# Gate and up projections as Strassen products over pairs of feed-forward tiles, in a two-layer decoder trunk

## The reference, cut to what matters

```python
D_MODEL, SEQ, DEPTH, N_META, D_FF = 1024, 1024, 2, 16, 2816
def swiglu(h, w_gate, w_up, w_down):
    return (jax.nn.silu(h @ w_gate) * (h @ w_up)) @ w_down
# h: 16 meta tokens, then the 1024 tokens of x
for layer in range(DEPTH):
    mix = attn_recurrent_mixer(h, ...) if layer % 2 == 0 else multiscale_pool(h, ...)
    h = layer_norm(ALPHA * h + mix, ln_mix_g[layer], ln_mix_b[layer])
    h = layer_norm(ALPHA * h + swiglu(h, w_gate[layer], w_up[layer], w_down[layer]), ln_ffn_g[layer], ln_ffn_b[layer])
return h[:, N_META:]
```

## Time and profile before

| | |
|---|---|
| median of 3 runs | 2736.35 us (2734.56 to 2738.01) |
| profiled execution, its own time | 2737.52 us |
| its span, first to last instruction | 2735.8 us |
| first gate/up matmul of the trunk | at 1060.1 us |
| last matmul of the last down projection | at 2716 us |
| mean granted TensorE clock | 0.96 of full speed |

### The profile page before, as it was taken

The page is one execution under the profiler, slowest core; times in us unless marked ns, Lnnn a source line. Parts: engine busy times, 40 slices in busy tenths (PEclk is TensorE's granted clock), DMA queues, the critical chain, the costliest instruction groups (busy, mean ns, idle before and its releaser), DMA issues.

```text
span 2735.8 us, 36593 instructions
## 1 busy us (share of the span) xinstructions
PE 2602.8 (95%) x14303; PEld 2217.5 (81%) x14303; DVE 1292.4 (47%) x2469; ACT 843.7 (31%) x1385; POOL 1077.6 (39%) x638
## 2 busy tenths in 40 slices
PE   7899999699999987999999999999999999999996
PEld 6789999668778876889888777888878788888885
DVE  6789995878776431333333332332322332232224
ACT  3674221333333222322222322322323232332221
POOL 1432222655444423443333433444434344445442
PEclk9999999689999998999999998999999999999998
DMA  3101220323322243232323322233323233333431
GB/s 129 32 17 58 91 74 13 100 85 105 93 85 91 72 142 116 70 93 78 101 71 92 93 75 79 77 99 101 92 62 93 64 90 108 93 94 107 119 105 47
DMA packets 276470, 232.96 MB, mean 85 GB/s; under 512 B 10448, under 2 KB 257296, under 8 KB 276304
## 3 DMA queue, kind: packets, MB, share of 16 engines
q1 hardware_dynamic: 268112, 222.13, 27.3%
q10 hardware_dynamic: 8192, 8.52, 0.9%
HBM read 217.91 MB, written 12.71 MB: 84 GB/s over the span
## 4 chain that ended last, share of the span: by engine, by line
PE 58%; DMA 1%; POOL 1%; ACT 1%; DVE 1%; issue 0%; POOLq 0%; SPq 0%; ACTq 0%; DVEq 0%
PE banks L1819 34%; PE banks L1835 19%; PE banks L1852 1%; PE banks L1857 1%; PE banks L1869 1%; DMA draw<-in_w_down 1%; PE banks L1543 1%; POOL wL L1738 1%; POOL dL L1745 0%; DMA raw<-in_w_up 0%; ACT wH L1913 0%; ACT dH L1919 0%; DVE y L2019 0%; DVE y L1521 0%; PE banks L1854 0%
## 5 line engine op out<-in xcount | busy, mean ns | idle before, releaser
L1738 POOL TENSOR_TENSOR wL<-raw,wH 128x2048 fp32r<-128x2048 f32 x88 | 406.3, 4617 | 596.2 <-ACT wH L1913 596.2
L1819 PE MATMUL banks<-hL,wH 128*128 128x512 f32 (+1 forms) x1760 | 620.4, 352 | 15.9 <-ACT hid L1928 13.5
L1819 PE MATMUL banks<-hH,wL 128*128 128x512 f32 (+1 forms) x1760 | 619.4, 352 | 0.0
L1819 PE MATMUL banks<-hH,wH 128*128 128x512 f32 (+1 forms) x1760 | 617.2, 351 | 0.0
L1999 DVE TENSOR_TENSOR hid<-hid,banks 128x512 f32<-128x512 f32 (+1 forms) x110 | 64.3, 585 | 759.6 <-PE banks L1819 654.8
L1819 PEld LDWEIGHTS banks<-hL,wH 128*128 128x128 f32 x1760 | 332.8, 189 | 65.4 <-ACT hid L1928 15.1
L1819 PEld LDWEIGHTS banks<-hH,wL 128*128 128x128 f32 x1760 | 332.7, 189 | 46.3
L1819 PEld LDWEIGHTS banks<-hH,wH 128*128 128x128 f32 x1760 | 333.2, 189 | 45.0
L1745 POOL TENSOR_TENSOR dL<-draw,dH 128x1024 fp32r<-128x1024 f32 x88 | 220.9, 2510 | 371.9 <-ACT dH L1919 371.8
L2019 DVE TENSOR_TENSOR y<-y,banks 128x512 f32<-128x512 f32 (+1 forms) x340 | 233.1, 686 | 219.8 <-PE banks L1835 218.8
L1835 PE MATMUL banks<-dH,hidL 128*128 128x512 f32 (+1 forms) x748 | 303.9, 406 | 2.3 <-issue 2.3
(11 more groups left out here) (235 smaller groups left out, 4316.4 us busy)
## 6 DMA issues: line engine op xcount, KB each, us to landing
raw<-in_w_gate SPq DMA_DIRECT2D x88, 512.0 KB, 4.7
raw<-in_w_up SPq DMA_DIRECT2D x88, 512.0 KB, 6.1
draw<-in_w_down SPq DMA_DIRECT2D x88, 512.0 KB, 3.5
w_out_part<-in_w_out SPq DMA_DIRECT2D x64, 512.0 KB, 4.0
va<-in_w_in SPq DMA_DIRECT2D x10, 1024.0 KB, 5.4
va<-in_x SPq DMA_DIRECT2D x8, 512.0 KB, 4.9
vg_scratch<-y ACTq DMA_DIRECT2D x32, 128.0 KB, 1.7
y<-in_x SPq DMA_DIRECT2D x8, 512.0 KB, 7.6
```

The source lines that it names most:

```text
L1738: nc.gpsimd.tensor_tensor(wL[:, ff % 2, :, :, :].rearrange("p g k f -> p (g k f)"), raw[:, :, :, :].rearrange("p g k f -> p (g k f)"), wH[ ...
L1819: last = nc.tensor.matmul(banks[:, GU + (2 * q + g) % 3, 0:n], wt[:, ff % 2, g, k, :], h[:, k, a:a + n], start=(k == 0 and part == 0), sto ...
```

## The change

For a pair of feed-forward tiles (f = 0, 1) and the two halves of a block's tokens (t), gate and up are each a 2x2 product over the two halves of the width: C[f][t] = A[f][0] B[0][t] + A[f][1] B[1][t]. Eight products of quarter size (four width slices, 264 or 256 tokens) become seven, in Winograd's form: four sums of weight quarters (S1 to S4, VectorE `sum_w`, both weights at once, 128x1024), four sums of token quarters (`sum_t`, once per block), and sums of the products on VectorE out of PSUM (`sum_c11` to `sum_c21`, with ScalarE's `keep_m1` copying the first product out). All seven operands of each side are split in high and low parts: seven `high_w` and `low_w` of 128x1024 per pair, through a ring of three, and seven token operands (`turn`, `high_op`, `low_op`) per block, made while the blocks change: some in the last pair of the old block ("early"), the rest in the first of the new ("late"). The silu now works in place on SBUF, and the multiplication with up (`mult`) has both inputs in SBUF. The meta tokens' halves are eight extra columns in block one, with small copies and subtractions of their own. Weights come as four quarters of a pair, eight transfers of 256 KB. The bands are made over pairs 2 to 8. TensorE's order: the first two products of a pair, the down projection of the pair before, the other five.

```diff
-        def gate_up(ff):
...
+        def bank_free(X):
+            if X < 0:
+                return
+            g, o, part = X // (2 * NO), X // 2 % NO, X % 2
+            pe.wait_ge((m1_kept, c11_made, u2_made, u3_made, u4_made, c12_made, c21_made)[o], 2 * g + part + 1)
...
+        def product(g, o):
...
+            for part in range(2):
+                X = 2 * n + part
+                bank_free(X - 3)
+                for k in range(HK):
+                    for t, (wt, h) in enumerate(((wH, hL), (wL, hH), (wH, hH))):
+                        last = nc.tensor.matmul(banks[:, GU + X % 3, 0:ph.n], wt[:, n % RING, part, k, :], h[:, o, k, 0:ph.n],
```

The order in TensorE's queue:

```diff
+            product(g, 0)
+            if when == "late":
+                turn(new, TO_S1)
+            product(g, 1)
...
+            for j in range(of_pair(g - 1)[0].NJ):
+                down(g - 1, j)
...
+            for o in range(2, NO):
+                product(g, o)
+                if when == "early" and o in (TO_S2, TO_S3):
+                    turn(new, o)
```

The order in ScalarE's queue:

```diff
+            keep_m1(g, 0)
+            keep_m1(g, 1)
+            high_w(g, TO_S2)
...
+            high_w(g, TO_S3)
+            silu(g, 0)
...
+            high_w(g, TO_S1)
...
+            high_hid(g, 0)
+            high_d(2 * g)
...
+            high_w(g, TO_S4)
...
+            high_w(g, TO_22)
...
+            silu(g, 1)
+            if g + 1 < NPAIR:
+                high_w(g + 1, TO_11)
+            high_hid(g, 1)
+            silu(g, 2)
+            if g + 1 < NPAIR:
+                high_w(g + 1, TO_21)
+            high_hid(g, 2)
+            high_d(2 * g + 1)
+            silu(g, 3)
+            high_hid(g, 3)
```

The order in VectorE's queue:

```diff
+            sum_w(g, 1)
+            sum_w(g, 2)
+            sum_w(g, 3)
...
+            sum_c11(g, 0)
...
+            sum_c11(g, 1)
+            mult(g, 0)
...
                 for j in range(of_pair(g - 1)[0].NJ):
                     add(g - 1, j)
+                    if j == 1:
+                        sum_w(g, 4)
...
+            low_hid(g, 0)
+            sum_u2(g, 0)
+            sum_u2(g, 1)
...
+            sum_u3(g, 0)
+            sum_u3(g, 1)
...
+            sum_c22(g, 0)
+            sum_u4(g, 0)
+            sum_c22(g, 1)
+            sum_u4(g, 1)
...
+            mult(g, 1)
+            sum_c12(g, 0)
+            low_hid(g, 1)
+            sum_c12(g, 1)
+            mult(g, 2)
+            sum_c21(g, 0)
+            low_hid(g, 2)
+            sum_c21(g, 1)
+            mult(g, 3)
...
+            low_hid(g, 3)
```

The order in POOL's queue:

```diff
+            low_w(g, TO_S2)
+            low_w(g, TO_S3)
+            low_w(g, TO_S1)
...
+            low_d(2 * g)
+            low_w(g, TO_S4)
+            low_w(g, TO_22)
+            if g + 1 < NPAIR:
+                low_w(g + 1, TO_11)
+                low_w(g + 1, TO_21)
             low_d(2 * g + 1)
```

The order in SP's queue:

```diff
+                sp.wait_ge(s_made, 4 * g + 4)
+                load_quad(g + 1, A11)
+                load_quad(g + 1, A12)
             load_d(2 * g + 1)
+            if g + 1 < NPAIR:
+                sp.wait_ge(w_lo, NO * g + TO_S4 + 1)
+                load_quad(g + 1, A21)
+                sp.wait_ge(w_lo, NO * g + TO_22 + 1)
+                load_quad(g + 1, A22)
                 load_d(2 * g + 2)
```

More of the change, by code:

```diff
@@ L1527, in bias @@
         self.nc.gpsimd.tensor_tensor(self.y[0:n, m, :], self.y[0:n, m, :], self.bb[0:n, :], ALU.add).then_inc(self.biased, 1)
[L1529 to L1563, removed]
@@ L1566 @@
-class Phase:
[L1569 to L1578, removed]
+TO_11, TO_21, TO_S2, TO_S3, TO_S1, TO_S4, TO_22 = range(7)
@@ L1585, in phases, with trunk @@
 def phases():
[L1586 to L1591, removed]
+    blocks = ((0, [0, 1, 2, 3, 4], (1, 3), 264), (0, [5, 6, 7, 8], (5, 7), 256),
+              (1, [1, 2, 3, 4], (1, 3), 256), (1, [5, 6, 7, 8], (5, 7), 256))
+    out, down = [], 0
+    for nth, (layer, tiles, half, n) in enumerate(blocks):
+        out.append(Phase(nth, layer, tiles, half, n, down))
+        down += out[-1].downs
     return out
-def trunk(nc, c, sem, sb, banks, ident, ins, y, hH, hL, out):
+def trunk(nc, c, sem, sb, banks, ident, ins, y, out):
     NW = len(POOL_WINDOWS)
@@ new lines, in down @@
+        def down(g, j):
+            ph, i = of_pair(g)
+            if j == 0:
+                pe.wait_ge(d_lo, 2 * g + 2)
+                pe.wait_ge(hid_lo, hids_to(g, 3))
+            m = ph.tiles[j // 2]
+            n = TILES[m][1]
+            num = ph.down(i, j)
+            if num >= 3:
+                pe.wait_ge(y_added, num - 2)
+            for u in range(2):
+                for part, (wt, h) in enumerate(((dH, hidL), (dL, hidH), (dH, hidH))):
+                    if m == 0:
+                        at = (metaL if h is hidL else metaH)[:, u, :]
+                    else:
+                        half = int(m >= ph.half[1])
+                        a = (m - ph.half[half]) * P
+                        at = h[:, u, half, a:a + P]
+                    last = nc.tensor.matmul(banks[0:n, DN + num % 3, :], at, wt[:, u, (j % 2) * 512:(j % 2 + 1) * 512],
+                                            start=(u == 0 and part == 0), stop=(u == 1 and part == 2))
+            last.then_inc(down_psum, 1)
@@ L1840, in pool_d, with turn_meta @@
+        def turn_meta():
+            for k in range(DC):
+                last = nc.tensor.transpose(banks[:, GU, k * N_META:(k + 1) * N_META], y[0:N_META, 0, k * P:(k + 1) * P],
+                                           ident[0:N_META, 0:N_META])
+            last.then_inc(meta_psum, 1)
         def pool_d(j):
@@ L1871, in pool_mix @@
             last.then_inc(mix_psum, 1)
-        for j in range(FIRST):
-            n0.turn(pe, j)
-        d_made, mixes, turns = [0], [0], [0]
+        d_made, mixes = [0], [0]
+        turn_meta()
+        turn(PH[0], TO_11)
         for g in range(NPAIR):
```

574 lines of the change are left out of this document (383 added, 191 removed).

## The result

The changed kernel takes 3000.11 us (median of four runs, 2986.20 to 3001.83) where the kernel before takes 2736.20 (four runs): a ratio of 1.095, 95% interval 1.0933 to 1.0966, 264 us slower. The profiled execution took 2999.37 us, its span 2997.7. The direction was forecast; the size was not, 103 us with a range to 2910.

A forecast was written before the change was run, and what follows sets the result against it. TensorE bounds the kernel before; after, VectorE's two-SBUF-input operations and POOL's subtractions exclude each other. Periods +40, norms +11, block 1 +10, block changes +36, end +6, start 0: +103, 2839 us; own range 2780 to 2875, with rivals 2700 to 2910.

The forecast's parts named there:

- the flat rule: Matmul spacing nearly flat in width: a half-width matmul costs about 0.75 of a full one, some 400 us more; 1 in 100.
- T: In a pair, counted from TensorE's start on the third product: end of VectorE's last low half of hid, 20.35 us.
- The period without the port: Feed-forward pair if VectorE's operations with two SBUF inputs and POOL's subtractions did not exclude each other (the port): 31.0 us.
- The step that failed: Down projection: the fourth weight sum waits for POOL's fourth low half, T+8.65; the third addition ends at T+10.45.
- the start: Stretch up to the first down projection: 0 us taken, bounds -20 and +10, beginning near 1112 as before.
- the averaged race: VectorE multiply ready 0.2 us after POOL has begun: period 35.05 us if lost, 34.2 if won; 34.6 taken.
- Pairs with norms: Norm pairs without pooling matmuls before the down projection, six in block 4, three in block 1: about +1.2 us, +11.
- Changes of block: Three changes, operands for the next block turned inside two pairs: 12 us each, bounds 6 and 15, +36.
- The end: End of the kernel: late additions 3.5 us and a longer chain from the last product 2.7, +6.
- The clock: Rival: TensorE's stands in down projections lower its clock in all 42 periods, +30 to +70 us, 2870 to 2910; chance 0.16.
- TensorE stays the bound: Rival: VectorE's waits fit between products, 2642 us (2620 to 2675); chance 0.19.
- waits half as long: Rival: VectorE's waits exist at half length, 32.8 us a period, some 2745 us, 2700 with fewer block-change losses; chance 0.10.

The follow-up runs named there:

- the second experiment: Changed kernel with POOL writing zeros for about as long in place of each weight low half from the fourth product on, reading no SBUF; 2777.68 us.
- The late fourth sum: Changed kernel with the fourth sum of weights moved behind all additions of the down projection; 2921.77 us.
- the first experiment: Changed kernel with POOL's low halves of the weights cut to 16 elements a row from the fourth product on; 2683.96 us.
- the best version: Changed kernel with late fourth sum, early first-quarter multiply, POOL's subtractions in halves, and change-of-block work and norms reordered; 2771.05 us, ratio 1.0123.
- The same kernel: Changed kernel with late fourth sum, early first-quarter multiply and POOL's subtractions in halves; 2805.58 us single, 2791.72 us in four runs.
- the two kernels without POOL's reads: Changed kernel and the best version, each with POOL's weight low halves cut to 16 elements from the fourth product on; 2683.96 and 2688.78 us.

## Why the prediction was wrong

**What held.** The matmul's spacing: the chain of the changed kernel has 9.98 us for 84 (0.119, forecast 0.118), so the flat rule of the Trainium skill falls here (TensorE: Matmul & The Clock Gate, Back-to-back issue gap: 81 ns at 128 columns, 131 at 512). The exclusion of POOL's subtractions and VectorE's operations with two SBUF inputs holds instruction by instruction, and an input in PSUM keeps an operation out of it. T and the first addition came within 0.2 us, and a blocked multiply and a low half each cost what POOL has left. The period without the port is 30.9 for 31.0. POOL's busy time stays inside the period (21.66 us), though the second experiment shows that it costs 94 us by its place in the order.

**The step that failed** is "the fourth sum ... waits for POOL's fourth low half, T+8.65; the third addition ends at T+10.45". The mechanism was the one named, its size was not. I let the sum begin at the end of the subtraction that releases it. But POOL had the next subtraction ready, and in the trace the sum begins 0.03 us after that end (that the time goes into the semaphore is my reading of it). So it was blocked by the next one: 2.17 us in 29 of the 44 pairs, 63 us, and 70 with the six shorter cases. The rule that I applied elsewhere (a multiply 0.2 us late is blocked) I did not apply where the end of the same POOL instruction is what releases VectorE. There it lost in all 29 cases. The late fourth sum gives back 2.1 us of the plain period.

That step is not the whole of the 161 us by which the sum was short. The lower clock, which the forecast left to a rival, is at most 64 of them, the start is 13, the averaged race 0.45 in each plain period, and the terms below are the rest; these overlap and can't be added up exactly.

**Mis-sized terms.** Pairs with norms: I put their extra at 1.2 us, and in block 4 it is 2.3 in the one pair in which the clock did not fall (39.7 us for 37.4) and 3.2 to 5.1 in the other four (40.6 to 42.5), which each hold 3.4 to 6.8 us at the lower clock. As I read it, POOL's `bias` delays its queue, so that it runs into the second multiply as well, and in pairs whose additions end late the norm stands in front of the drains; no run isolates either. The start: 0 forecast, +13.4 measured, 3.4 above the upper bound. Transposes and splits in turn stop TensorE 2.37 us each, but that is not the loss: the first experiment has the same stops, stands 3.54 us for the first drain where the changed kernel stands 6.89, and begins the first down projection at 1112.5, as the kernel before; with POOL writing it is 1113.5. So these 13 us too are the exclusion. Changes of block: +12 each and the period's own excess, 43 in all, for 51.9. The end: 6 for 10.

**The clock** was a rival (0.16) and is a part of the result. TensorE stood 1.31 and 2.64 us in the down projection shown. From 1056 us on it spends 232 us at the lower of its levels (1.2 of 2.4 GHz), for 104 before, by the granted clock in the trace; the two long stretches above agree (0.06 and 0.03 of their length lost are 233 and 101 us at half). The period in which it fell has a mean of 0.92 and takes 40.3 for 37.4 us, with the same two stands as the one before it, in which it didn't fall. 128 us more at half rate are at most 64 us of lost time. In the first experiment, nearly without gaps, it is 107, as before. So the clock is at most a quarter of the 264 us, and it goes away with the waits. The fall of the earlier trace rows, which the prediction gave 5 us, lasts 10.2 (1607.9 to 1618.1 at 0.50), 5 of them in the down projection; TensorE had not stood in the 60 us before it.

**Rivals.** "TensorE stays the bound" and "waits half as long" are out (the second's own terms give 2748, not 2745). The interval was too narrow above: every delay that I found in the plain pair I repeated 42 times, but I did not ask what a schedule misses, and each miss here lengthens. The clock was priced as another case, though the forecast's own gaps make it likely: the two should have been added, for some 2890 (2839 and the rival's 30 to 70).

## What to carry to other kernels

Before giving VectorE and POOL more work with all inputs in SBUF, add up the time in which they exclude each other, but do not take a sum below the period for a sign that it fits: with in-order queues the loss comes from each collision, at up to one whole POOL instruction, and it went on to 264 us with 29 of 31 us used. Cut POOL's instructions short before reordering anything (138 us here for a change in two places), and never put a VectorE operation that is released by a POOL instruction in front of something urgent while POOL's next is ready. Taking work off the busiest engine (here an eighth of the gate and up products) is worth what the others leave of it: here about 2% without the exclusion, and nothing in any version that computes the whole.

## What was not expected of the hardware

- An operation of VectorE that is released by the end of a POOL subtraction lost to POOL's next one in all 29 pairs where that was ready (3.38 us for 1.22), where one that was already waiting gets in (1.17 us at 2856.85, ending 0.3 us after the first of POOL's three).
- Two POOL instructions of 512 elements cost 1409 ns each on average, against 2450 for one of 1024: 15% more in sum (11% in the best version, at 1365); the kernel still gained 138 us.
- POOL writing only, by memsets, does not lengthen VectorE's operations with two SBUF inputs (0.42 to 0.48 us for the multiplies, 1.21 to 1.23 for the 79 sums of weights that ran beside one).
- The same kernel differed by 14 us between two chips in single and repeated runs (2805.58, 2791.72), while the kernel before differed by 4; the time at the lower clock, 191 and 164 us, differs enough for it.
- Not tried: the old order in the first pair alone (the rearrangement costs 12 us ahead of the first down projection: 1124.8 for 1112.5 in the two kernels without POOL's reads), and POOL's subtractions in quarters.
